# Mixer projections as blocks of 512 columns in two K halves, a forget gate with stationary weights, and a new order of columns and norms

## The reference

```python
def token_mixer(h, w_in, fox_forget_b, ...):          # first block, w_in is 1024 x 3080
    proj = h @ w_in
    fq, fk, fv, fgate, dq, dk, dv = jnp.split(proj, IN_SPLITS, axis=-1)   # 512,512,512,8,512,512,512
    log_f = jax.nn.log_sigmoid(fgate + fox_forget_b)
    c = jnp.cumsum(log_f, axis=1)                      # decay added to the fox scores
    fox_o = causal_block_attention(fq, fk, fv, c)      # 8 heads of 64
    ...                                                # differential attention: 4 heads, q and k twice
    return jnp.concatenate([fox_o, diff_o], axis=-1) @ w_out

def hybrid_mixer(h, w_in, w_gate, ...):               # second block, w_in 1024 x 2752, w_gate 1024 x 3072
    (sb_q, sb_k, sb_v, nq, nkc, nvc, nks, nvs, nkw, nvw, ngate,
     dq, dk, dv, iq, ik, iw) = jnp.split(h @ w_in, offs, axis=-1)
    o_a = stick_breaking_attention(sb_q, sb_k, sb_v)   # 4 heads ("sb")
    o_b = nsa_attention(nq, ...)                       # 8 heads; q, k_sel, k_win: rms_norm, then rope
    o_c = dsa_attention(dq, dk, dv, iq, ik, iw, ...)   # 4 heads; q, k: rms_norm, then rope; k shared
    g_a, g_b, g_c = jnp.split(jax.nn.sigmoid(h @ w_gate), 3, axis=-1)
    merged = g_a * (o_a @ w_br_a) + g_b * (o_b @ w_br_b) + g_c * (o_c @ w_br_c)
    return merged @ w_out
```

## Time and profile before

| | |
|---|---|
| three runs | 1778.76, 1778.35, 1777.59 us (median 1778.35) |
| the profiled execution | 1777.57 us, its span 1775.6 us |
| mean granted TensorE clock | 0.994 |
| busy: PE, DVE, ACT, POOL | 98%, 57%, 47%, 6% of the span |
| chain that ended last | PE 86%, ACT 5%, DVE 4%, issue 3%, POOL 1% |
| DMA | 300.03 MB, mean 169 GB/s |

### The profile page before, as it was taken

The page is one execution under the profiler, slowest core; times in us unless marked ns, Lnnn a source line. Parts: engine busy times, 40 slices in busy tenths (PEclk is TensorE's granted clock), DMA queues, the critical chain, the costliest instruction groups (busy, mean ns, idle before and its releaser), DMA issues.

```text
span 1775.6 us, 24998 instructions
## 1 busy us (share of the span) xinstructions
PE 1745.5 (98%) x9810; PEld 1503.3 (85%) x9810; DVE 1017.6 (57%) x1415; ACT 841.6 (47%) x1142; POOL 104.9 (6%) x136
## 2 busy tenths in 40 slices
PE   8999999999999999999999999999999999999999
PEld 6888898788888888899988888888888999888887
DVE  5445545755466445667677544554456676775454
ACT  5444455644445344465464444443444654644442
POOL 1000200100003000010001000020000100010000
PEclk9999999999999999999999999999999999999999
DMA  8454543265456555434344554564544343445542
GB/s 290 184 195 176 165 125 112 103 225 190 183 195 220 190 202 177 143 97 141 120 140 149 210 198 180 190 222 188 210 167 142 107 132 119 143 150 206 204 174 95
DMA packets 99002, 300.03 MB, mean 169 GB/s; under 512 B 6353, under 2 KB 65937, under 8 KB 73697
## 3 DMA queue, kind: packets, MB, share of 16 engines
q1 hardware_dynamic: 96320, 291.66, 46.3%
q0 software_dynamic: 2592, 7.12, 1.4%
HBM read 297.71 MB, written 1.05 MB: 168 GB/s over the span
## 4 chain that ended last, share of the span: by engine, by line
PE 86%; ACT 5%; DVE 4%; issue 3%; POOL 1%; DMA 0%; SPq 0%; ACTq 0%
PE ps L539 12%; PE ps L537 12%; PE ps L538 12%; PE ps L601 9%; PE ps L603 9%; PE ps L602 9%; PE ps L810 4%; PE ps L811 4%; PE ps L812 4%; ACT w_hi L251 3%; PE ps L585 2%; ACT p_buf L929 2%; PE ps L558 1%; PE ps L559 1%; PE ps L348 1%
## 5 line engine op out<-in xcount | busy, mean ns | idle before, releaser
L258 DVE TENSOR_TENSOR w_lo<-raw,w_hi 128x2048 fp32r<-128x2048 f32 x276 | 625.6, 2285 | 279.2 <-ACT w_hi L251 278.8
L251 ACT ACTIVATE w_hi<-raw 128x2048 fp32r<-128x2048 f32 x276 | 520.5, 1906 | 25.6 <-PE ps L603 24.8
L537 PE MATMUL ps<-w_hi,aT_hi 128*128 128x512 f32 x960 | 379.6, 395 | 0.0
L539 PE MATMUL ps<-w_hi,aT_lo 128*128 128x512 f32 x960 | 374.7, 390 | 0.0
L538 PE MATMUL ps<-w_lo,aT_hi 128*128 128x512 f32 x960 | 374.0, 390 | 0.0
L695 ACT ACTIVATE tmp<-ps,stats 128x256 f32<-128x256 f32 x132 | 62.0, 474 | 573.9 <-PE ps L539 556.9
L810 PE MATMUL ps<-w_hi,aT_hi 128*128 128x256 f32 (+1 forms) x848 | 251.2, 296 | 7.2 <-ACT proj L854 7.2
L736 DVE TENSOR_TENSOR tmp<-tmp,ps 128x256 f32<-128x256 f32 x132 | 55.3, 422 | 340.4 <-ACT tmp L695 340.4
L812 PE MATMUL ps<-w_hi,aT_lo 128*128 128x256 f32 (+1 forms) x848 | 243.1, 287 | 0.0
L811 PE MATMUL ps<-w_lo,aT_hi 128*128 128x256 f32 (+1 forms) x848 | 243.1, 287 | 0.0
L539 PEld LDWEIGHTS ps<-w_hi,aT_lo 128*128 128x128 f32 x960 | 180.2, 188 | 38.3
(11 more groups left out here) (296 smaller groups left out, 1821.7 us busy)
## 6 DMA issues: line engine op xcount, KB each, us to landing
raw<-in_ffn_units SPq DMA_DIRECT2D x197, 1024.0 KB, 4.8
raw<-in_w_in SPq DMA_DIRECT2D x34, 1024.0 KB, 5.4
raw<-in_w_gate SPq DMA_DIRECT2D x24, 1024.0 KB, 5.1
raw<-in_w_out SPq DMA_DIRECT2D x12, 1024.0 KB, 4.9
qk_t<-in_nsa_cmp_w POOLq DMA_DIRECT2D x8, 512.0 KB, 5.6
raw<-in_w_br_b SPq DMA_DIRECT2D x4, 1024.0 KB, 4.8
raw<-in_w_br_a SPq DMA_DIRECT2D x2, 1024.0 KB, 4.8
raw<-in_w_br_c SPq DMA_DIRECT2D x2, 1024.0 KB, 4.9
```

What stands on the lines that cost most here:

```text
L251: nc.scalar.activation(w_hi[w][:, 0:width], raw[k][:, 0:width], ACT.Copy).then_inc(hi_ready, 1)
L258: nc.vector.tensor_tensor(w_lo[w][:, 0:width], raw[k][:, 0:width], w_hi[w][:, 0:width].bitcast(F32), ALU.subtract).then_inc(lo_ready, 1)
L537: nc.tensor.matmul(dst, aT_hi[:, a, toks], hi[:, k, :], start=a == 0, stop=False)
L539: last = nc.tensor.matmul(dst, aT_lo[:, a, toks], hi[:, k, :], start=False, stop=a == KC - 1)
```

## The change

Mixer projections are cut in blocks of 512 columns. A block is two units, K chunks 0 to 3 and 4 to 7. PE works in quarters (one tile, one K half: 12 matmuls of 512 columns). PSUM bank 0 holds tile 0's block and bank 1 tile 1's. ACT copies out each tile's block by itself: tile 0's waits for the new semaphore `proj_t0`, tile 1's for `unit_used`; each waits for its own tile's rstd alone. One block of mix2, the last of `w_in`, stays 256 columns wide with all K chunks.

```diff
@@ projections, PE and ACT
-        def pe_cols(pe, n, w, bank, evacuated, tiles=(0, 1), between=None):
-            if evacuated > 0 and tiles[0] == 0:
-                pe.wait_ge(proj_evac, evacuated)
+        def pe_quarter(pe, ph, blocks, b, t, h, between=None):
+            first, _, w = blocks[b]
+            n = ph["u0"] + first + (h if w == 512 else 0)
+            if h == 0:
+                pe.wait_ge(proj_evac, 2 * (ph["block0"] + b - 1) + t + 1)
             pe.wait_ge(lo_ready, n + 1)
...
+            dst, toks = ps[:, t, 0:w], slice(t * P, (t + 1) * P)
+            for a in range(h * KC // 2, (h + 1) * KC // 2):
...
+            if t == 0 and h == 1:
+                last.then_inc(proj_t0, 1)
...
+        def act_evac(act, ph, blocks, b, t, pieces):
+            first, _, w = blocks[b]
+            if t == 0:
+                act.wait_ge(proj_t0, ph["block0"] + b + 1)
+            else:
+                act.wait_ge(unit_used, ph["u0"] + first + w // 256)
```

At every entry the first token tile's squares move in front of the copy of the second transposed tile, on ACT:

```diff
@@ act_boundary
-            split_hi(act, prev["u_end"] + 2, width=width_of(prev["u_end"] + 2))
+            split_hi(act, prev["u_end"] + 2)
+            act_prenorm(act, ph, 0)
             act_transposed(act, ph["t0"], 1)
             split_hi(act, prev["u_end"] + 3)
-            for t in range(NT):
-                act_prenorm(act, ph, t)
+            act_prenorm(act, ph, 1)
```

```diff
@@ mix1
-        cols1 = [(Q0, 256), (K0, 256), (GATE0, FH), (Q0 + 256, 256), (K0 + 256, 256), (V0, 256), (V0 + 256, 256),
-                 (DIFF0, 256), (DIFF0 + 512, 256), (DIFF0 + 256, 256), (DIFF0 + 768, 256),
-                 (DIFF0 + 1024, 256), (DIFF0 + 1280, 256)]
+        blocks1 = [(0, Q0, 512), (2, K0, 512), (4, V0, 512), (6, DIFF0, 512), (8, DIFF0 + 512, 512),
+                   (10, DIFF0 + 1024, 512)]
...
+        def pe_forget(pe):
+            pe.wait_ge(sem("forget_split"), 1)
+            for k in range(KC):
+                nc.tensor.matmul(dst, hi[:, k, :], aT_hi[:, k, :], start=k == 0, stop=False)
+                nc.tensor.matmul(dst, lo[:, k, :], aT_hi[:, k, :], start=False, stop=False)
+                last = nc.tensor.matmul(dst, hi[:, k, :], aT_lo[:, k, :], start=False, stop=k == KC - 1)
...
-            for i in range(2, 6):
-                unit(i)
+            pe_enter_mixer(pe, ph)
+            pe_forget(pe)
+            tile(1, 0)
+            pe_forget_transposes(pe)
+            tile(1, 1)
+            tile(2, 0)
...
@@ attention fillers and splits of mix1 (PE, ACT)
-                    unit(8 + i // 2, (i % 2,))
+                    j = i + 2
+                    pe_quarter(pe, ph, blocks1, 3 + j // 4, j % 4 // 2, j % 2)
...
-                if i % 2 == 0:
-                    ahead(8 + i // 2)
-                else:
-                    evac1(act, ph, 8 + i // 2)
+                if i < 3:
+                    ahead(7 + i)
+                if i % 2:
+                    evac1(act, ph, 3 + (i + 1) // 4, (i + 1) % 4 // 2)
```

In mix2 the columns come in another order, the norms too ("first", "second", "dsa"), and the transposes of all normed heads are one group that waits for all three:

```diff
@@ mix2
-        cols2 = [2304, DIN - 256, 1280, 0, 256, 512, 2048, 768, 1024, 1536, 1792]
+        blocks2 = [(0, DIN - 512, 512), (2, 1024, 512), (4, 0, 512), (6, 512, 512), (8, 1536, 512), (10, DIN - 768, 256)]
+        gate_blocks = [(N_IN + 2 * i, 512 * i, 512) for i in range(6)]
...
@@ pe_mix2
-            unit(10)
+            tile(6, 0)
+            wait(pe, "qk_first_ready", ph)
+            wait(pe, "qk_second_ready", ph)
             wait(pe, "dk_ready", ph)
-            wait(pe, "qk_first_ready", ph)
-            pe_items(pe, st, qk_items_1, 4)
-            unit(11)
-            wait(pe, "qk_second_ready", ph)
+            pe_items(pe, st, qk_items, 4)
+            quarter(6, 1, 0)
             pe_items_left(pe, st)
-            pe_items(pe, st, qk_items_2, 4)
...
             def beside(i, place):
-                if i <= 10:
-                    unit(12 + i, (place,))
-                elif place == 0:
+                j = 2 * i + place + 3
+                if j < 24:
+                    quarter(6 + j // 4, j % 4 // 2, j % 2)
+                elif place == 0 and i > 10:
...
@@ dve_mix2
-            qk_normed(0, qk_dsa, "qk_dsa_ready")
-            ahead(9)
+            ahead(10)
+            qk_normed(1, qk_second, "qk_second_ready")
+            qk_sums(2, qk_dsa)
+            dve.wait_ge(proj_evac, pj0 + 12)
...
+            qk_normed(2, qk_dsa, "qk_dsa_ready")
             wait(dve, "qk_dsa_ready", ph)
             nc.vector.tensor_copy(dk_twice..., ...).then_inc(ev("dk_ready", ph)[0], 1)
-            qk_normed(1, qk_first, "qk_first_ready")
```

More of the change, by code:

```diff
@@ L846, in a_chunks, with pe_tile, pe_enter_mixer, part @@
+        def pe_tile(pe, ph, blocks, b, t, between=None):
+            for h in range(2):
+                pe_quarter(pe, ph, blocks, b, t, h, between)
+        def pe_enter_mixer(pe, ph):
+            def part(kh, t, between=None):
+                mm = pe_gate_up_part(pe, ph, t, kh, between, bank=0)
+                if t == 1:
+                    mm.then_inc(unit_used, 1)
+                elif kh == 1:
+                    mm.then_inc(proj_t0, 1)
+            pe_enter(pe, ph, part)
         def a_chunks(i):
@@ new lines, in pe_forget_transposes, with act_forget_copy @@
+        def pe_forget_transposes(pe):
+            pe.wait_ge(sem("forget_copied"), 1)
+            for t in range(NT):
+                c = S + t * FH
+                last = nc.tensor.transpose(ps[:, FORGET_BANK, c:c + FH], forget_sb[:, t * P:(t + 1) * P],
+                                           ident[0:FH, 0:FH])
+            last.then_inc(sem("forget_t_done"), 1)
+        def act_forget_copy(act):
+            act.wait_ge(sem("forget_done"), 1)
+            nc.scalar.activation(forget_sb, ps[0:FH, FORGET_BANK, 0:S], ACT.Copy).then_inc(sem("forget_copied"), 1)
@@ L1233, in sp_mix1, with act_forget_evac @@
+        def act_forget_evac(act, ph):
+            act.wait_ge(sem("forget_t_done"), 1)
+            for t in range(NT):
+                c = S + t * FH
+                nc.scalar.activation(gate_z[:, t, :], ps[:, FORGET_BANK, c:c + FH], ACT.Copy, scale=rstd(ph, t))\
+                    .then_inc(sem("gate_z_ready"), 1)
         def sp_mix1(sp, ph):
             w_in, w_out = A["w_in"][0], A["w_out"][0]
-            for i, (c0, w) in enumerate(cols1):
-                sp_cols(sp, ph["u0"] + i, w_in, c0, w)
+            for block in blocks1:
+                sp_block(sp, ph["u0"], block, w_in)
@@ L1426, in dve_mix1 @@
                 if i == 0:
[L1427 removed]
+                    ahead(11)
                 if 1 <= i <= DH:
@@ L1748, in hidden @@
                     mm.then_inc(ev("hidden_ready", ph)[0], 1)
-            pe_enter(pe, ph, lambda i, t, between=None: pe_cols_part(pe, ph, i, t, between))
-            unit(2)
+            pe_enter_mixer(pe, ph)
+            tile(1, 0)
             wait(pe, "ik_ready", ph)
             pe_items(pe, st, ix_items, 4)
-            unit(3)
+            tile(1, 1)
             pe_items_left(pe, st)
             ix_logits(0)
+            quarter(2, 0, 0)
+            pe.wait_ge(proj_evac, pj0 + 4)
             for a in range(2):
@@ L1778, in pe_mix2 @@
             pe_sb_scores(pe, 1, ph)
-            unit(7)
+            tile(4, 0)
             wait(pe, "hid_ready", ph)
@@ L1784, in pe_mix2 @@
                 .then_inc(ev("kcvc_ready", ph)[0], 1)
-            unit(8)
+            tile(4, 1)
             for half_ in range(2):
@@ L1943, in act_mix2 @@
                                      ACT.Exp).then_inc(sem("sb_w_ready"), 1)
-            unit(9)
+            evac(5, 0)
+            evac(5, 1)
+            act.wait_ge(proj_evac, 2 * ph["block0"] + 12)
+            squares(qk_dsa[0])
+            ahead(10)
+            wait(act, "gates_clamped", ph)
+            nc.scalar.activation(nsa_gate, nsa_gate, ACT.Exp, scale=-1.0).then_inc(ev("gates_exp", ph)[0], 1)
             wait(act, "kcT_psum", ph)
@@ L2288, in _ @@
                 after = next_of(ph)
+                if after and after["kind"] == "mix1":
+                    pool_mix1_loads(pool)
                 if after and after["kind"] == "mix2":
```

421 lines of the change are left out of this document (212 added, 209 removed).

## The result

The changed kernel is slower: median 1786.44 us of six runs against 1778.16 of six of the kernel before, ratio 1.0044, 95% interval 1.0031 to 1.0057. Its profiled execution took 1786.28 us, 8.7 more than the one before. Each hybrid mixer is parted at the first score of its attention.

A forecast was written before the change was run, and what follows sets the result against it. TensorE bounds the kernel, busy 98% of the span with 86% of the chain. Mix1 -10.0 and two hybrid mixers at +3.0 each (+6.0) sum to -4.0 on 1777.57: 1773.6 us; own range 1768 to 1778, overall 1761 to 1782.

The forecast's parts named there:

- Mix1, -10.0: Mix1: entry wait -1.4, gate -5.5, half clock behind it -1.5, units -2.1 and -0.3, new clock drops +0.8.
- the offset that the prediction took for nought: Fox attention: split moved forward costs +1.9, the iteration it left gets as much shorter; ends +4.2 and -2.5.
- Entry of the hybrid mixers, -7.2: Each hybrid mixer up to its norms: entry wait -2.75, half clock behind it -1.5, ten units -3.0.
- Three quarters in front of the attention, +2.4: Each hybrid mixer, first sb output to first score: 20.68 us instead of 18.26, with more projection work there.
- the wait for `dk_ready` 6.3: Before each hybrid mixer's head transposes: series of 14.6 us behind the last block, less 8.3 of PE cover.
- its clock 2.1: Behind each hybrid mixer's `dk_ready` wait: half of 4.28 us at lower clock lost, +2.1; alternatives 1.5 and 4.4.
- The loop behind it does not give this back: Hybrid mixers' attention: ACT and DVE set the pace; PE's two fillers shrink 0.15 each to no use.
- the same 9.3 a batch: Sign to check: the hybrid mixers' attention keeps its pace of 9.3 us a batch.
- the -0.6: Hybrid mixers' attention: PE leads only in the first iteration and a half, four shorter fillers there save 0.6 us.
- Rival R2: Hybrid mixers: POOL's power takes 4.88, longer wait (+2.9) and low clock (+2.1) each; 1783.6 us, slower; chance 0.16.
- The rule of the Trainium skill: Warm matmul costs columns plus some 2.5 ns; halving the number saves 0.06 a unit, not 0.30; 1782.0 us; chance 0.02.
- the forecast's 44%: Stretches at half clock: in 3.35 us matmuls took 0.21 instead of 0.12, so 44% of such time is lost.

The follow-up runs named there:

- mix1 alone: Mix1 as in the changed kernel, both hybrid mixers as in the kernel before but with the earlier squares at entry: 1764.19 us, ratio 0.9926 to the kernel before.
- the fox splits: Changed kernel with fillers put back, DVE's norm and sums before the split, and fox attention's splits in iterations one, three, five: 1762.28 us, ratio 0.9919.
- the dsa block earlier: Changed kernel with fillers, DVE norm order and old fox split places, plus dsa columns' block before the last 512 and dsa norm first: 1763.24 us, ratio 0.9912.
- The first run: New mix1 with both hybrid mixers as in the kernel before, except the earlier squares at entry: 1764.19 us, ratio 0.9926 to the kernel before.
- the run with the order on DVE: Changed kernel, but DVE does the second group's norm and the dsa sums before the next unit's split: 1776.73 us, ratio 0.9991 to the kernel before.
- quarters reordered: Changed kernel, but from the eighth block quarters run both tiles per half, and ACT copies both tiles before even iterations: 1776.84 us, ratio 0.9990.
- the fillers put back: Changed kernel, but the quarter in front of the hybrid mixers' attention goes back into it, filling every place: 1774.45 us, ratio 0.9979.
- the last run: New mix1 with fox splits in the first, third and fifth iteration, hybrid mixers old but for the earlier squares: 1758.47 us, ratio 0.9890.

## Why the prediction was wrong

By its steps:

- *Mix1, -10.0.* Right: -10.97. The entry wait is gone, the gate takes 2.75 (2.9 forecast) at full clock, and the fox attention is as long as before, 40.74 against 40.81. With the same code the other profiled executions have mix1 at -7.7 to -10.9. It hides one loss, though, the offset that the prediction took for nought. Without any half clock in it the fox attention took 40.8 us with the three splits in a row (mix1 alone) and 38.7 with the old places (the fox splits; the dsa block earlier), so the row costs 2.0. With half clock in it it took 40.7 to 42.3 with the row and 40.4 with the old places (the last run). The kernel before, at 40.81, had a wait of 1.18 and 3.4 us of half clock behind it, and so did not show this.
- *Entry of the hybrid mixers, -7.2.* Right: from the entry to the end of the same ten units it is about 6.8 less. The first run shows that the earlier squares alone give 3.8.
- *Three quarters in front of the attention, +2.4, the wait for `dk_ready` 6.3 and its clock 2.1.* Right: +4.4 and +3.7 together with the entry, wait 5.75; behind the ten units it is 11.2 more in the first mixer, where 10.8 were forecast, and the run with the order on DVE shows the series as the cause. The low clock lasted 6.8 us, not 4.3; most of it fell on transposes.
- *"The loop behind it does not give this back. Its pace is ACT's and DVE's ... while PE's two fillers shrink by 0.15 each to no use."* This step failed. It is true of PE's matmuls, that they are not what sets the pace: from the attention on it takes 143.7 us with blocks of 512 (quarters reordered) and 143.6 with units of 256 (mix1 alone). But the prediction took from it that PE's fillers can't hurt, and priced only their length. They also ask for units. PE had been moved one place ahead of ACT and DVE, and the block's order asks for two new units in two successive places, with the splits coming one per iteration. Four waits a mixer, 5.4 us, came from that, and either edit alone, the fillers put back or the quarters reordered, takes them away. Of the forecast's signs the one on this step failed, "the same 9.3 a batch": from the fourth score batch to the fifth, with the wait of 2.75 and 3.4 us of half clock in it, the first mixer took 13.1 us (834.57 to 847.69), where it took 9.0 before. Between the first and the last score it is only 1.0 longer (80.96 against 79.95), as other iterations were shorter than before; the last of these waits and the hole behind it come after.
- *The end of the hybrid mixers' attention* was not priced at all; the sum has only the -0.6. The quarter taken out in front left the last filler place empty, a hole of 2.7 to 2.9 us in front of PE's last outputs, and the clock was low at it for 3.4 us in one mixer and 6.8 in the other. That is half of the difference between the two mixers, +3.6 and +6.8. The other half is the 3.4 us at the half clock from 1525.4 on, behind the last wait for a split, which only the second mixer has: from the last score to the end of the hole it takes 18.8 us in the first and 20.4 in the second, and 46.9 and 48.5 from there to the end of the stage. What decides whether and how long the clock falls there was not tried.

Rival R2 had the right sign and a wrong place: the power took 1.95, not 4.88, and the wait for `dk_ready` was no longer than forecast. The range, up to 1782, left R2's 1783.6 out, and no case had the hybrid mixers' attention dearer than before. A slip that changes no step: the forecast of 1773.6 is 4.0 below the profiled execution, and the "4.8 below the median" of the runs adds the 0.8 by which the profiled execution lay under that median, though the saving is 4.0 on either scale. The rule of the Trainium skill that the prediction weighed had no part in it: the starts of the changed blocks stand 0.227 apart as the earlier trace rows has them.

Against the form with the old hybrid mixers the recast ones bring nothing even then, and rather cost (1762.28 and 1758.47, with the same mix1). What 512 columns save in front of the attention, the remaining wait for the dsa norm and its clock take: to the first score 100.1 and 100.9 us against 99.4 and 99.9, and from there, where most of the low clock behind that wait falls, 144.8 and 146.1 against 143.6 in both.

## What to carry to other kernels

A filler beside a loop that other engines pace is not free because it is short: it takes buffers at the moment it runs. Before moving one, write down for each place which unit it needs first and when that unit's last producer ends; with PE one place ahead, an order that asks for two in successive places waited 5.4 us a mixer here, and one that asks for one every second place did not wait. And where work is taken from a loop's end to its start, look at what the engine does in the last place.

A wait of PE has a price behind it. Of the changed kernel's nine waits of 1.75 us and more in the mixers, eight had a stretch of 3.4 or 6.8 us at half clock at them. One of 3.4 loses some 1.5 us by the forecast's 44%, an estimate, so that a wait of 2.75 us is worth some 4.2, which the 13.1 us against 9.0 above bear out.

## What the runs showed of the hardware

- In a stream of 8-column matmuls at 0.111 us each, with 128-column weights, the granted clock fell to 0.50 after 4.3 us with no wait in front of it (one execution); in 24 matmuls of 256 columns with 8-column weights, 2.75 us long, it did not.
- With 8 columns of weights 256-column matmuls started 0.115 apart (2.75 / 24), with 128 columns of weights 0.1195.
- POOL's power takes longer when it begins just behind a unit split of DVE. Alone, the power took 1.65 us on 8 columns, 1.95 to 2.00 on 10 and 2.94 on 16 (in the changed kernel). With a split begun 0.16 before it, it took 3.93 on 10 (DVE's order changed) and 4.88 on 16 (before; the maximum of the earlier trace rows). Both are 1.94 to 1.98 more, and the split's own 2.28 or 2.29 stays. With the dsa block earlier it is another case: the power on 8 columns began 0.83 before the split, lay beside it for 0.81, and took 1.64, and the split 2.29, neither any longer. There are two calls of each kind in an execution, the profile's spans on POOL are rough, and no experiment was made on it alone. The Trainium skill, "GPSIMD Engine Reference", section "Specifications", says that GpSimd shares its SBUF interfaces with VectorE and that a VectorE instruction with two SBUF inputs, as the split is, contends. The trace agrees where the split came first, with 1.94 to 1.98 us on POOL's side; where the power came first it shows nothing of it.
